# Experts on 96 rows in 64- and 32-column products, with interleaved input weights and two result buffers

## The reference

```python
def _hier_moe(h, p):
    gl = (h @ p['w_group_router']).astype(jnp.float32)
    g_sel = jax.nn.one_hot(jnp.argmax(gl, axis=-1), N_GROUPS, dtype=jnp.float32)
    ...
    top_v, top_i = lax.top_k(el_sel, TOP_K)
    ...
    for gi in range(N_GROUPS):
        a = jnp.einsum('bsd,edf->bsef', h, p['w_e1'][gi])
        b = jnp.einsum('bsd,edf->bsef', h, p['w_e3'][gi])
        y = y + jnp.einsum('bsef,efd->bsd', jax.nn.silu(a) * b * w_all[:, :, gi, :, None], p['w_e2'][gi])
    return y
```

## Time and profile before

| | us |
|---|---|
| median of 3 runs | 2262.74 |
| lowest, highest | 2257.99, 2264.68 |
| the profiled execution | 2261.1 |
| its span, first to last instruction | 2259.4 |

### The profile page before, as it was taken

One profiled execution on the slowest core, in us unless ns is written; L12 is line 12 of the kernel. 1 busy time (PEld: TensorE's weight loads), 2 busy tenths in 40 slices (PEclk: granted clock), 3 DMA queues, 4 the chain that ended last, 5 costly groups with the idle time before them and its releaser, 6 DMA issues.

```text
span 2259.4 us, 23696 instructions
## 1 busy us (share of the span) xinstructions
PE 2156.4 (95%) x9730; PEld 1190.5 (53%) x9730; DVE 699.3 (31%) x1861; ACT 483.6 (21%) x926; POOL 69.8 (3%) x97
## 2 busy tenths in 40 slices
PE   6999999999999889999989999999999988999997
PEld 3445556566555544444445565656655544444443
DVE  1373664333211301010144677533421121000014
ACT  3211233344100201011023123334410021001011
POOL 0000100000000100000010010000000011000001
PEclk9999999999999999999999999999999989999999
DMA  9666562212124468888732212122222345888873
GB/s 382 264 244 243 206 213 78 86 57 112 58 110 184 158 234 356 336 351 319 286 140 75 112 46 114 43 81 98 76 93 112 124 173 218 326 351 320 351 276 140
DMA packets 45983, 426.17 MB, mean 189 GB/s; under 512 B 5424, under 2 KB 5552, under 8 KB 19760
## 3 DMA queue, kind: packets, MB, share of 16 engines
q1 hardware_dynamic: 38880, 400.99, 45.5%
q0 software_dynamic: 6992, 23.61, 3.0%
HBM read 389.96 MB, written 34.61 MB: 188 GB/s over the span
## 4 chain that ended last, share of the span: by engine, by line
PE 93%; DMA 3%; DVE 2%; issue 1%; ACT 1%; SPq 0%; DVEq 0%; ACTq 0%
PE psum L1125 20%; PE psum L741 15%; PE psum L1024 15%; PE psum L1134 10%; PE psum L1039 7%; PE psum L744 6%; PE psum L1067 4%; PE psum L662 2%; PE psum L855 1%; DMA ring<-wmod_in 1%; DMA ring<-wch_in 1%; PE psum L1115 1%; PE psum L719 1%; PE psum L806 1%; PE psum L1154 1%
## 5 line engine op out<-in xcount | busy, mean ns | idle before, releaser
L741 PE MATMUL psum<-hT,ring 128*128 128x384 f32 x1088 | 367.6, 491 | 2.0 <-ACT pc L1304 1.9
L1024 PE MATMUL psum<-hT,ring 128*128 128x384 f32 x1024 | 343.2, 488 | 0.0
L741 PEld LDWEIGHTS psum<-hT,ring 128*128 128x128 f32 x1088 | 202.4, 191 | 143.1 <-issue 17.4
L1024 PEld LDWEIGHTS psum<-hT,ring 128*128 128x128 f32 x1024 | 192.3, 190 | 131.1
L1125 PE MATMUL psum<-ring,scr 128*128 128x512 f32 x512 | 225.6, 599 | 14.6 <-issue 14.6
L1125 PE MATMUL psum<-pc,scr 128*128 128x512 f32 x512 | 222.6, 593 | 0.0
L1039 PE MATMUL psum<-pc,ring 128*128 128x384 f32 x512 | 175.6, 486 | 0.0
L2155 DVE TENSOR_TENSOR scr<-scr,psum 128x512 f32<-128x512 f32 x32 | 22.0, 688 | 476.8 <-ACT scr L1565 476.8
L1125 PEld LDWEIGHTS psum<-ring,scr 128*128 128x128 f32 x512 | 97.3, 193 | 131.6 <-issue 131.6
L1722 DVE SCALAR_TENSOR_TENSOR pc<-pc,par 128x128 f32<-128x128 f32 x480 | 159.5, 414 | 0.0
L1125 PEld LDWEIGHTS psum<-pc,scr 128*128 128x128 f32 x512 | 96.2, 190 | 115.9 <-issue 115.7
(11 more groups left out here) (333 smaller groups left out, 1943.2 us busy)
## 6 DMA issues: line engine op xcount, KB each, us to landing
ring<-we_in SPq DMA_DIRECT2D x48, 2048.0 KB, 12.5
pc<-we_in SPq DMA_DIRECT2D x48, 2048.0 KB, 12.6
ring<-wmod_in SPq DMA_DIRECT2D x42, 1024.0 KB, 5.9
ring<-wch_in SPq DMA_DIRECT2D x18, 2048.0 KB, 9.4
ring<-wgate_in SPq DMA_DIRECT2D x16, 2048.0 KB, 8.1
ring<-wbr_in SPq DMA_DIRECT2D x16, 1024.0 KB, 8.0
expert_out_rows<-scr SPq DMA_DIRECT2D x30, 512.0 KB, 13.3
ring<-wtok_in SPq DMA_DIRECT2D x6, 2048.0 KB, 8.4
```

The lines of the kernel that those rows point to most:

```text
L741: mm = pe.matmul(F[:, 0:T], wv[:, k, n * P:(n + 1) * P], hT[:, k, :], start=k == 0, stop=k == KD - 1)
L1024: mm = pe.matmul(bank(5 + n % 2)[:, 0:T], wv[:, k, (n % 4) * P:(n % 4 + 1) * P], hT[:, k, :], start=k == 0, stop=k == KD - 1)
```

## The change

An expert now has CAP = 96 slots in both tables, of which BIG = 64 and SUB = 32 are computed apart. All tests against P = 128 are made against 96.

- `hidden`: for the first 64 rows, 16 products with 64 stationary and 512 moving columns, the two blocks of weights in turn: block 0 fills partitions 0 to 63 of bank 2, block 1 partitions 64 to 127. For the last 32 rows, 32 products with 32 stationary and 256 moving columns, each quarter of the 1024 weight columns in 32 partitions of bank 3.
- The host interleaves w_e1 and w_e3 by 128 columns, so that each block has two pieces of both, and silu and multiplication work on one view, `x_ab`, of 128 x 384 elements, where they had 128 x 512.
- `turn_hidden` has 3 transposes for 4, `turn_rows` 8 of 96 columns.
- `project` makes the 1024 output columns of 64 rows in 2 x 4 products of 512 columns (bank 5), and those of 32 rows in 4 x 4 products of 256 columns (bank 6). Expert 15 keeps the whole form, with 96 rows.
- `x_y` is two buffers of 128 x 768, and a copy waits for the store before the last. A store is now two transfers, whose destinations take the partitions in 2 groups of 64 rows and in 4 groups of 32.

```diff
+CAP, BIG = 96, 64
...
+        x_y = [scr[:, 768 * (i + 1):768 * (i + 2)] for i in range(2)]
...
                 def store_rows(e):
                     sp.wait_ge(xy_ready.sem, xy_ready.at(l, 2 * e + 2))
-                    sp.dma_start(ys_d[e * P:(e + 1) * P, :], x_y).then_inc(y_stored.sem, 16)
+                    sp.dma_start(ys_d[e * CAP:e * CAP + BIG, :].rearrange("t (h n) -> h t n", h=2), x_y[e % 2][:, 0:W])\
+                      .then_inc(y_stored[e % 2].sem, 16)
+                    sp.dma_start(ys_d[e * CAP + BIG:(e + 1) * CAP, :].rearrange("t (q n) -> q t n", q=4), x_y[e % 2][:, W:768])\
+                      .then_inc(y_stored[e % 2].sem, 16)
...
-                    for j in range(2):
-                        w = have(l, ("exp", e, j))
-                        for k in range(KD):
-                            mm = pe.matmul(bank(2 + j), x_h[:, k, :], w[:, k, :], start=k == 0, stop=k == KD - 1)
+                    w = [have(l, ("exp", e, j)) for j in range(2)]
+                    for k in range(KD):
+                        for h in range(2):
+                            pe.matmul(bank(2)[BIG * h:BIG * h + BIG, :], x_h[:, k, 0:BIG], w[h][:, k, :],
+                                      start=k == 0, stop=k == KD - 1, skip_group_check=True)
+                    for k in range(KD):
+                        for c in range(4):
+                            part = slice(c % 2 * 256, c % 2 * 256 + 256)
+                            mm = pe.matmul(bank(3)[SUB * c:SUB * c + SUB, 0:256], x_h[:, k, BIG:CAP], w[c // 2][:, k, part],
+                                           start=k == 0, stop=k == KD - 1, skip_group_check=True)
...
+                        size, lo, width = ((BIG, 0, 512), (SUB, BIG, 256))[n]
+                        for c in range(P // size):
+                            mm = pe.matmul(bank(5 + n)[size * c:size * c + size, 0:width], x_gT[:, f, lo:lo + size],
+                                           w2[:, f, c * width:(c + 1) * width], start=f == 0, stop=f == 3,
+                                           skip_group_check=True)
...
-                        if n == 0 and e >= 1:
-                            ve.wait_ge(y_stored.sem, y_stored.at(l, e * 16))
-                        ve.tensor_copy(x_y[:, n * W:(n + 1) * W], bank(5 + n)).then_inc(xy_ready.sem, 1)
+                        if n == 0 and e >= 2:
+                            ve.wait_ge(y_stored[e % 2].sem, y_stored[e % 2].at(l, e // 2 * 32))
+                        width = (W, 256)[n]
+                        ve.tensor_copy(x_y[e % 2][:, n * W:n * W + width], bank(5 + n)[:, 0:width]).then_inc(xy_ready.sem, 1)
```

More of the change, by code:

```diff
@@ L306, in hybrid_step @@
         d_wt = scr[:, 1920:2304]
[L309 to L313, removed]
+        x_h = scr[:, 0:KD * CAP].rearrange("p (k n) -> p k n", k=KD)
+        x_y = [scr[:, 768 * (i + 1):768 * (i + 2)] for i in range(2)]
+        x_last = scr[0:CAP, 768:768 + D]
+        x_s, x_g = (scr[:, c:c + 3 * P].rearrange("p (a f) -> p a f", a=3) for c in (2304, 2688))
+        x_gT = mva_flat[:, 0:4 * CAP].rearrange("p (c n) -> p c n", c=4)
+        x_rows = [mva_flat[0:CAP, 512:1536], pc_flat[0:CAP, 12288:13312]]
+        x_ab = psum[1][:, 0:6 * P].rearrange("p (a s f) -> p a s f", a=3, s=2)
+        x_turned = psum[0][:, :].rearrange("p (k n) -> p k n", k=KD)[:, :, 0:CAP]
         y_a = [vals[:, t * D:(t + 1) * D] for t in range(NT)]
@@ L440, in hybrid_step @@
         xy_ready = sig("expert_out_ready", 2 * NE)
-        y_stored = sig("expert_out_stored", (NE - 1) * 16)
+        y_stored = [sig(f"expert_out{i}_stored", (NE // 2 - i) * 32) for i in range(2)]
         back_in = [sig(f"back_rows{t}_in", 32) for t in range(NT)]
@@ L1139, in turn_hidden @@
                     pe.wait_ge(xg_ready.sem, xg_ready.at(l, e + 1))
-                    for f in range(4):
-                        mm = pe.transpose(bank(4)[:, f * P:(f + 1) * P], x_g[:, f * P:(f + 1) * P], ident)
-                    mm.then_inc(xgt_done.sem, 1)
+                    turned = bank(4)[:, 0:4 * CAP].rearrange("p (c n) -> p c n", c=4)
+                    pairs = bank(4)[:, 0:4 * CAP].rearrange("p (h j n) -> p h j n", h=2, j=2)
+                    for j in range(2):
+                        pe.transpose(pairs[:, :, j, 0:BIG], x_g[:, j, :], ident)
+                    pe.transpose(turned[:, :, BIG:CAP], x_g[:, 2, :], ident).then_inc(xgt_done.sem, 1)
                 def turn_mix(t):
@@ L1172, in _ @@
                     with pe.Fori(0, NE) as i:
-                        w1 = ring[3].rearrange("p (k n) -> p k n", k=KD)
-                        w3 = ring[4].rearrange("p (k n) -> p k n", k=KD)
+                        w13 = [ring[3 + j].rearrange("p (k n) -> p k n", k=KD) for j in range(2)]
                         w2 = ring[5].rearrange("p (c n) -> p c n", c=4)
@@ L1229, in _ @@
                         pe.wait_ge(out_used.sem, out_used.at(l, KD + n - 1))
-                    pe.matmul(bank(n % 2)[:, 0:T], x_y[:, n * P:(n + 1) * P], last_pickT, start=True, stop=True)\
+                    pe.matmul(bank(n % 2)[:, 0:T], x_last[:, n * P:(n + 1) * P], last_pickT[0:CAP, :], start=True, stop=True)\
                       .then_inc(out_done.sem, 1)
@@ L1564, in _ @@
                         ac.wait_ge(xg_ready.sem, xg_ready.at(l, e))
-                    ac.activation(x_s, bank(2), ACT.Silu).then_inc(xs_ready.sem, 1)
+                    ac.activation(x_s, x_ab[:, :, 0, :], ACT.Silu).then_inc(xs_ready.sem, 1)
                     if e + 1 < NE:
@@ L2205, in zero_rows @@
                 gp.dma_start(xs_d.rearrange("(p s) (a n) -> p (s a) n", p=P, n=256),
-                             zeros[:, :].rearrange("p (a n) -> p a n", a=1).to_broadcast([P, NE * 4, 256]))\
+                             zeros[:, :].rearrange("p (a n) -> p a n", a=1).to_broadcast([P, NE * CAP // P * 4, 256]))\
                   .then_inc(rows_zeroed.sem, 16)
@@ L2384 @@
         "wout": np.concatenate([_by_partition(inputs["w_out"][l], W) for l in L]),
-        "we13": np.concatenate([_by_partition(inputs[k][l, e // EPG, e % EPG], W)
-                                for l in L for e in range(NE) for k in ("w_e1", "w_e3")]),
+        "we13": np.concatenate([_by_partition(_paired(*(inputs[k][l, e // EPG, e % EPG] for k in ("w_e1", "w_e3"))), W)
+                                for l in L for e in range(NE)]),
         "we2": np.concatenate([_by_partition(inputs["w_e2"][l, e // EPG, e % EPG], D) for l in L for e in range(NE)]),
@@ L2393 @@
     args += [nc.dram_tensor(f"{n}_out", s, F32, kind="ExternalOutput").ap() for n, s in outputs.items()]
-    args += [nc.dram_tensor(f"{n}_rows", (NE * P, D), F32, kind="Internal").ap() for n in ("expert_in", "expert_out")]
+    args += [nc.dram_tensor(f"{n}_rows", (NE * CAP, D), F32, kind="Internal").ap() for n in ("expert_in", "expert_out")]
     hybrid_step(nc, *args)
```

49 lines of the change are left out of this document (28 added, 21 removed).

## The result

| | before | after |
|---|---|---|
| median | 2263.15 | 2291.13 |
| lowest, highest | 2257.99, 2264.68 | 2287.67, 2297.38 |
| the profiled execution | 2261.1 | 2293.54 |
| its span | 2259.4 | 2291.8 |

Both columns are in us, of four runs each. The ratio is 1.0131, with a 95% interval from 1.0102 to 1.016: the kernel is slower by 1.3%, 23 to 36 us. The forecast was 2282, with 65% on slower.

A forecast was written before the change was run, and what follows sets the result against it. TensorE bounds the kernel before, one loaded DMA engine after. A layer sums -16 + 15.4 - 1.5 + 10 = +7.9 us, both +15.8; layer 0's small weights add 5.5: +21.3, 2282 us, range 2245 to 2340.

The forecast's parts named there:

- What bounds the kernel before: Expert stage before the change: TensorE alone makes the chain, 21.91 us a period, with the DMA engines busy for 0.87.
- Products: `hidden` and `project`: side-by-side products cut them to 10.3 and 5.15 us, TensorE's period to 17.6 us.
- Dealing by outermost steps, both stores on a common engine: Expert stores: outermost steps 2 and 4 use two and four engines; one engine carries 160 KB, 6.6 us.
- The loaded engine's 23.3 us: Expert loop: the most loaded DMA engine sets the period at 23.3 us, between 22.3 and 25.6.
- The 0.9 us allowed for an engine that lags: Loaded engine's period: half of a 1.7 us loss seen where all engines begin together, range 0.0 to 1.7.
- Nothing queued behind it that is late by as little: SyncE's queue: one more transfer an expert costs 0.3 us of issue and delays nothing behind it.
- Four periods at TensorE's pace, -16 us: Start of each layer's loop: the loads' lead lets about four periods run at TensorE's pace, 4 x -4.0 us.
- Layer 0's small weights and parameters, 5.5 us: Layer 0: these loads, 141 KB for each engine, add 5.5 us that the free 13% took before.
- The end, +10 a layer: End of each layer: gathers wait for the loaded engine's last transfers, token sums start at about 25 us, +10.
- The start of layer 0, 0: Up to layer 0's first `hidden`: no change in time, 0 us.
- TensorE waits for `we_in`: Sign in the loop: TensorE waits for DMA `we_in` from about the fifth expert on, period near 23.3 us.
- Rival A, 2143 us: Stores spread over all 16 engines: transfers need 18.4 us a period; 2143 us, between 2120 and 2165, chance 0.13.

The follow-up runs named there:

- e12: e5 with whole products of 96 stationary columns, as for expert 15, in place of the side-by-side ones: 2251.03 us, ratio 0.9938.
- e9: The changed kernel with the rows' load issued ahead of the weights and the second store cut into four transfers for all 16 engines: 2236.82 us, ratio 0.9862.
- e10: The changed kernel with rows loaded ahead of weights and the second store cut into two transfers of outermost step 2 each: 2307.31 us, ratio 1.0184.
- e6: The changed kernel with only the next rows' load issued ahead of the weights, stores unchanged: 2271.45 us, ratio 1.0001.
- e1: The changed kernel with both stores cut into six transfers, one per partition group, spread over all 16 engines: 2178.84 us, ratio 0.9602.
- e5: e1 with the next rows' load issued ahead of the weights: 2160.76 us, ratio 0.9519.
- e7: The changed kernel with both stores, patterns unchanged, issued by ScalarE instead of SyncE: 2302.64 us, ratio 1.0143.

## Why the prediction was right, and where it wasn't

- **What bounds the kernel before: right.** With the whole products and light transfers (e12) the period is TensorE's 21.6 us, near the 21.9 of before.
- **Products: right.** 10.7 us for 10.3 in `hidden`, 5.5 for 5.15 in `project`, 17.35 a period for 17.6. Each part was too low by 3 to 7%, and the 1.0 us that the sum added apart for six changes of width made up for it. By the ratio that the Trainium skill states (TensorE: Matmul & The Clock Gate, Measured speedup vs the span model) the estimate was 21.7 us a period; that ratio is not what these shapes show, with 17.35.
- **Dealing by outermost steps, both stores on a common engine: right.** The packets and the share of 0.13 show 2 and 4 engines, e9 and e10 that one of them carries both stores. Which engine it is, no record shows.
- **The loaded engine's 23.3 us: right in size, partly for another reason.** The stores' term was 6.6 and measured 6.9. The 0.9 us allowed for an engine that lags stood for nothing of the kind: with the rows first the period is 22.5, the sum without it. The last 0.8 come with the issue order, most likely by the ring of rows, holds and low clock, which the forecast did not have. That 0.9 allowed and 0.8 missed are nearly the same is luck.
- **"Nothing queued behind it that is late by as little": wrong.** It priced SyncE's issues at 0.3 us. In 19 of 30 cases the issue of the second store takes 7 to 22 us, and the next expert's rows and weights stand behind them. The step took the issue of a transfer for a fixed cost. That changed little here, most likely because the engine behind the hold was the bound itself.
- **Four periods at TensorE's pace, -16 us: too much in layer 1.** The first four periods took 1969.45 - 1895.87 = 73.6 us, where those of before took 1961.65 - 1878.38 = 83.3: -9.7 (the forecast's own 17.6 and 21.9 us would give 4.3 a period, and it took 4.0 without saying why). One of them was 24.4 us long. With the rows first it is 17.3, so what was missed is again the rows behind 4 MB of weights. In layer 0 the four periods gave -14.2.
- **Layer 0's small weights and parameters, 5.5 us: too little.** Ten periods of 24.25 us against 23.27 in layer 1 are 10 us. In e6 and e9, with the rows first, a single period of layer 0 is longer, by 5.8 and 4.5 us, which is what was counted. That the ring doubles the cost is likely, but no run takes it apart.
- **The end, +10 a layer: right.** The gathers start 16.8 us after the start of the last copy, with 18 forecast, and the first token sum 25.3 us after that of its first half, with "about 25" forecast (the earlier trace rows has 15.0):

```profile
1133.12 0.69 DVE L2134 COPY scr<-psum 128x512 f32<-128x512 f32 x1 [4.31 <-PE psum L1154]
1135.02 0.42 DVE L2134 COPY scr<-psum 128x256 f32<-128x256 f32 x1 [1.20 <-PE psum L1154]
...
1158.43 0.75 DVE L2190 TENSOR_SCALAR vals<-vals,rt 128x1024 f32<-128x1024 f32 x1 [11.73 <-DMA ring<-expert_out_rows,slot_back]
```

```profile
1151.78 1.06 POOL L2287 DMA_INDIRECT vals<-expert_out_rows,slot_back  x1 [367.19 <-issue]
```

- **The start of layer 0, 0: -5.0 us here.** The kernels with the change, alike up to this place, start that `hidden` anywhere from 791.0 to 797.1 us, so these 5 us can't be put down to the change.
- **"TensorE waits for `we_in`": wrong as a sign, right as a cause.** It waited for the rows, whose transfer was the last in the same full queue.
- **Rival A, 2143 us: would have been too low by 36.** e1 is that rival. Its mean period was 18.8 us for 18.4, in which two or three of each layer are much longer than the rest (21.7 to 25.7 us), and its end costs 3 to 5 us a layer where it was given -3. Only with the rows first (2161) does it come into A's range. The 18.4 us for the transfers were too many: e5 moves the same bytes in 17.35. And 21.9 - 18.4 is 3.5 us a period, not 3.6, which is 3 us in all.

The sum, then, was 21 us, the profiled execution 32 and the medians 28. The two loops were under-priced by 14 us and the ends by 2, and 5 us came back at the start.

## What to carry to other kernels

Before a store is rearranged, read the outermost step of its pattern: here 2 and 4 steps put it on 2 and 4 DMA engines, and 32 or more on all 16. A mean share of 0.80 says nothing of the one engine that is full; sum the bytes of each engine over a period and take the largest. Where SyncE's issues last long in the trace, look for a transfer on few engines just ahead, and put what is small and needed soon ahead of what is large and needed late. Here these two edits turn a loss of 1.3% into a gain of 4.8%.

## What the runs showed of the hardware that was not expected

**A transfer on few engines holds the engine that issues the next one.** An issue takes 0.3 to 0.6 us as a rule. In the changed kernel 40 of 300 take over 3 us, 368 us in all, the longest 21.85; in e7 ScalarE is held for up to 32.87. A busy queue alone doesn't do it: in e1 and e5, with all 16 engines busy at a share of 1.01, none of 420 issues takes over 2.6 us. Nor does the pattern of the held transfer: in e9, where the second store is spread, its issues still take up to 22.17 us behind the first store on two engines. What the issuing engine lacks meanwhile the trace doesn't show.

**The DMA share doesn't tell the rate.** Stretches of e1 and of e5, layer 1:

```profile
1900.00:2050.00 150.00, 139.10 (x1226) 57.55 (x1224) 13.36 (x24) 14.35 (x24) 0.00 (x0) 0.98 1.01 377
```

```profile
1900.00:2050.00 150.00, 150.00 (x1317) 61.48 (x1313) 14.47 (x26) 14.81 (x25) 0.00 (x0) 1.00 1.01 399
```

Both have all engines busy, and the one with the rows first moves 6% more; weights alone made 429 at the same share. By the trace's records, from 1900 to 2100 us, the packets of 4 KB (the rows in) take 255 ns in e1 and 202 in e5 on average, those of 16 KB (weights) 684 and 647. Why the order changes that is open.

**Short waits can cost clock.** After a wait of 6.16 us `turn_rows` took 1.54 us, at a granted clock of 0.50 (877.0 to 878.8 us; 1.2 of 2.4 GHz), and `project` 7.60; after one of 1.59 us they took 0.88, at 1.00 (853.5 to 854.5 us), and 5.52. The first half of `hidden` took 8.4 to 10.1 us behind waits of 2.8 in e6 and e10, and 7.09 behind none in e5. The length of the wait alone doesn't decide it: in the rows of e9 above, `hidden` took 8.78 us behind a wait of 2.80 and 7.09, at a granted clock of 1.00, behind one of 2.82. Over the loop of layer 1 the granted clock was 0.91 in the changed kernel (1900 to 2100 us) and 1.00 in e5. In a loop that a transfer bounds, the lost clock is hidden as long as nothing of the transfer waits for TensorE; in the chain of the changed kernel the rows' issue does.
